# Stick-breaking attention on halves of the TensorE array, with a cap on VectorE for the longest key block

## The reference

```python
z = jnp.einsum('bhqd,bhkd->bhqk', qi, k) * scale
mask = s_idx[None, :] < t_idx[:, None]
log_beta = jax.nn.log_sigmoid(z)
log_one_minus = jnp.where(mask, jax.nn.log_sigmoid(-z), 0.0)
tail = lax.cumsum(log_one_minus, axis=-1, reverse=True) - log_one_minus
a = jnp.where(mask, jnp.exp(log_beta + tail), 0.0)
o = jnp.einsum('bhqk,bhkd->bhqd', a, v)
```

## Time and profile before

| | before |
|---|---|
| median of 3 runs | 1307.05 us (1306.72 to 1307.06) |
| the profiled execution | 1307.16 us, its span 1305.4 us |
| busy in the span: TensorE, VectorE, ScalarE, GpSimd | 98%, 58%, 49%, 26% |
| granted TensorE clock | 0.999 of 2.4 GHz |
| first S to first matmul of `out1` | 501.49 to 626.29 us, 124.80 us |

### The profile page before, as it was taken

One profiled execution on the slowest core, in us unless ns is written; L12 is line 12 of the kernel. 1 busy time (PEld: TensorE's weight loads), 2 busy tenths in 40 slices (PEclk: granted clock), 3 DMA queues, 4 the chain that ended last, 5 costly groups with the idle time before them and its releaser, 6 DMA issues.

```text
span 1305.4 us, 17841 instructions
## 1 busy us (share of the span) xinstructions
PE 1285.4 (98%) x6478; PEld 1072.7 (82%) x6478; DVE 751.5 (58%) x1201; ACT 641.7 (49%) x1164; POOL 344.6 (26%) x393
## 2 busy tenths in 40 slices
PE   7999999999999999999999999999999999999998
PEld 6997778788888888888888888888888888888876
DVE  5656889735652235898454653334475434578843
ACT  5379787724532334998244432513343333357632
POOL 2228877400000007774000000000000000479720
PEclk9999999999999999999999999999999999999999
DMA  5232100122222232001223233332223322321111
GB/s 192 82 113 65 45 19 20 49 97 97 97 97 97 97 97 81 17 0 32 97 97 97 80 98 97 97 97 81 79 87 99 120 97 71 122 78 37 50 65 65
DMA packets 70867, 104.66 MB, mean 80 GB/s; under 512 B 3476, under 2 KB 31368, under 8 KB 70664
## 3 DMA queue, kind: packets, MB, share of 16 engines
q1 hardware_dynamic: 69584, 99.44, 24.2%
q0 software_dynamic: 1088, 4.17, 1.0%
q10 hardware_dynamic: 120, 0.05, 0.0%
HBM read 101.55 MB, written 2.10 MB: 79 GB/s over the span
## 4 chain that ended last, share of the span: by engine, by line
PE 89%; DVE 5%; issue 2%; ACT 2%; DMA 1%; SPq 0%; DVEq 0%; POOL 0%; ACTq 0%; POOLq 0%
PE ps L496 24%; PE ps L498 24%; PE ps L497 24%; PE ps L700 3%; PE ps L858 2%; PE ps L713 1%; PE ps L950 1%; PE ps L679 1%; PE ps L1009 1%; PE ps L848 1%; PE ps L727 1%; PE ps L849 1%; DVE sp L2093 1%; PE ps L728 1%; DMA x_tok<-in_x 1%
## 5 line engine op out<-in xcount | busy, mean ns | idle before, releaser
L1696 DVE TENSOR_TENSOR w_lo<-stage,w_hi 128x1024 fp32r<-128x1024 f32 (+4 forms) x188 | 223.9, 1191 | 416.0 <-ACT w_hi L1115 415.7
L1115 ACT ACTIVATE w_hi<-stage 128x1024 fp32r<-128x1024 f32 (+4 forms) x188 | 191.0, 1016 | 457.8 <-PE ps L498 457.1
L496 PE MATMUL ps<-a0h,w_hi 128*128 128x512 f32 x512 | 203.9, 398 | 1.1 <-DVE q_lo L2280 0.8
L498 PE MATMUL ps<-a0h,w_lo 128*128 128x512 f32 x512 | 199.8, 390 | 0.0
L497 PE MATMUL ps<-a0l,w_hi 128*128 128x512 f32 x512 | 199.5, 390 | 0.0
L2381 POOL TENSOR_TENSOR small<-small 128x16 f32<-128x16 f32 (+2 forms) x14 | 32.3, 2312 | 387.9 <-DVE small L1774 284.4
L496 PE MATMUL ps<-w_hi,a0h 128*128 128x512 f32 (+1 forms) x320 | 121.9, 381 | 0.1
L498 PE MATMUL ps<-w_hi,a0l 128*128 128x512 f32 (+1 forms) x320 | 119.9, 375 | 0.0
L497 PE MATMUL ps<-w_lo,a0h 128*128 128x512 f32 (+1 forms) x320 | 119.8, 374 | 0.0
L496 PEld LDWEIGHTS ps<-a0h,w_hi 128*128 128x128 f32 x512 | 96.2, 188 | 20.8 <-DVE w_lo L1696 1.3
L498 PEld LDWEIGHTS ps<-a0h,w_lo 128*128 128x128 f32 x512 | 96.1, 188 | 20.4
(11 more groups left out here) (331 smaller groups left out, 2807.1 us busy)
## 6 DMA issues: line engine op xcount, KB each, us to landing
stage<-in_a_w_in SPq DMA_DIRECT2D x48, 512.0 KB, 3.7
stage<-in_ple_w_gate SPq DMA_DIRECT2D x16, 512.0 KB, 3.3
stage<-in_w_kv_shared SPq DMA_DIRECT2D x16, 512.0 KB, 3.6
stage<-in_sb_w_in SPq DMA_DIRECT2D x16, 512.0 KB, 3.7
stage<-in_a_w_out SPq DMA_DIRECT2D x16, 512.0 KB, 3.4
stage<-in_b_w_in SPq DMA_DIRECT2D x16, 512.0 KB, 3.7
stage<-in_mla_w_in SPq DMA_DIRECT2D x8, 512.0 KB, 3.8
stage<-in_sb_w_out SPq DMA_DIRECT2D x8, 512.0 KB, 3.3
```

The source lines that it names most:

```text
L496: pe.matmul(bank, wh, mh, start=start and not seeded, stop=False, skip_group_check=seeded)
L498: return pe.matmul(bank, wl, mh, start=False, stop=stop, skip_group_check=seeded)
L1115: act.activation(slab(w_hi[r % 2], L, nk, w), slab(stage[r % 4], L, nk, w), ACT.Copy).then_inc(S("hi_ready"), 1)
L1696: dve.tensor_tensor(slab(w_lo[r % 2], L, nk, w), slab(stage[r % 4], L, nk, w), slab(w_hi[r % 2], L, nk, w), ALU.subtract)\
```

## The change

- **S on row halves.** The split operands go. A block's score is one f32 matmul over 64 rows, and the four blocks of a head alternate between the upper and the lower 64 rows of the array. Two of the four need the head's keys and queries on the other 64 partitions; SyncE copies these by DMA within SBUF (`swap`, four copies of 64x512 a pair). Blocks j=3 and j=2 write the same bank, so j=2 waits for j=3 (`row_done`). The masking matmuls come after all four blocks, two of them merged into one, and each block waits by itself for the W that frees its bank (`a_done` now counts three per head).
- **V on column halves.** Both heads of a pair go into one bank by f32 matmuls with 64 columns of `v_sh` each, the two heads in turn, block by block. V runs once a pair; TensorE's order is T(2i), V(i-1), S(2i+2), T(2i+1), S(2i+3).
- **The cap.** For the longest block ScalarE's abs goes. VectorE writes min(z, 40) (`soft_cap`), ScalarE takes exp(+x) and ln(1+x), and VectorE forms max(min(that, 20), z).
- **Around it.** W waits bank by bank; one gate a pair; the split of its result moves to GpSimd (`sb_parts`), which also issues the loads of `p_tok` and `ws_tok` later; `sp_h` and `sp_l` have two buffers; the loops are written out.

```diff
+EXP_MOST, LOG_MOST = 40.0, 20.0
...
+        def swap(pair):
+
+            if pair < 4:
+                sp_.wait_ge(S("sb_q_read"), pair + 1)
+            if pair > 2:
+                sp_.wait_ge(S("sb_q2_read"), 4)
+            if pair > 1:
+                sp_.wait_ge(S("z_done"), 4 * (pair - 1))
+            for t, to in zip((kT_sh, qT_sb), swapped(pair)):
+                for s in range(2):
+                    sp_.dma_start(to[head_rows(s), :], t[head_rows(s, True), pair, :]).then_inc(S(f"swapped{pair % 2}"), 16)
...
+                    if r == end_load("sb_q2") - 1:
+                        swap(0)
+                        swap(1)
+                    if r == lin["out1"].load0 + 3:
+                        swap(2)
+                    if r == lin["out1"].load0 + 4:
+                        for pair in range(3, PAIRS):
+                            swap(pair)
...
+        def sb_scores(h):
+
+            pair, s = h // 2, h % 2
+            k_other, q_other = swapped(pair)
+            pe.wait_ge(S("sb_q_read"), min(pair + 1, 4))
+            if pair > 3:
+                pe.wait_ge(S("sb_q2_read"), pair - 3)
+            pe.wait_ge(S(f"swapped{pair % 2}"), 64 * (pair // 2 + 1))
+            for n, (j, half) in enumerate(((3, 0), (1, 1), (0, 0), (2, 1))):
                 b, c = KEY_BANK[j]
-                n = T - j * P
-                bank = ps[3 * s + b]
-                kk, qq = slice(j * P, (j + 1) * P), slice(j * P, T)
-                pe.matmul(bank[:, c:c + n], kb[:, kk], qb[:, qq], start=j != 2, stop=False, skip_group_check=True)
-                pe.matmul(bank[:, c:c + n], kb[:, kk], ql[:, qq], start=False, stop=False, skip_group_check=True)
-                t = pe.matmul(bank[:, c:c + P], ident_r[:, :], strict_r[:, :], start=False, stop=False, skip_group_check=True)
-                if j < 2:
-                    t.then_inc(S("z_done"), 1)
-
-        def sb_tails(h, s, first=False):
-
+                rows = head_rows(half)
+                k = kT_sh[rows, pair, j * P:(j + 1) * P] if half == s else k_other[rows, j * P:(j + 1) * P]
+                q = qT_sb[rows, pair, j * P:T] if half == s else q_other[rows, j * P:T]
+                if h > 1 and n < 3:
+                    pe.wait_ge(S("a_done"), 3 * (h - 2) + (n + 1))
+                if j == 2:
+                    pe.wait_ge(S("row_done"), h + 1)
+                t = pe.matmul(ps[3 * s + b][:, c:c + T - j * P], k, q, start=j != 2, stop=False, skip_group_check=True)
+                if j == 3:
+                    t.then_inc(S("row_done"), 1)
+            pe.matmul(two_blocks(ps[3 * s + 2]), ident_r[:, :], twice(strict_r), start=False, stop=False, skip_group_check=True)
+            for b in (1, 0):
+                pe.matmul(ps[3 * s + b][:, 0:P], ident_r[:, :], strict_r[:, :], start=False, stop=False, skip_group_check=True)\
+                    .then_inc(S("z_done"), 1)
+
+        def sb_tails(h, first=False):
+
+            s = h % 2
...
+                if j < MB - 1:
+                    t.then_inc(S("tail_done"), 1)
...
-                t = pe.matmul(ps[6 + s][:, j * P:T], v_pair2[:, j, :], a_T[s][:, KEY_COL[j]:KEY_COL[j] + T - j * P],
-                              start=j == 0, stop=j == MB - 1, skip_group_check=True)
+                for s in range(2):
+                    c = i * P + s * HD
+                    t = pe.matmul(ps[6 + i % 2][head_rows(s), j * P:T], v_sh[:, j, c:c + HD], attend(i, s, KEY_COL[j], T - j * P),
+                                  start=j == 0, stop=j == MB - 1, skip_group_check=True)
             t.then_inc(S("o2_done"), 1)
...
+        for i in range(1, PAIRS):
+            sb_tails(2 * i)
+            sb_values(i - 1)
+            if i < PAIRS - 1:
+                sb_scores(2 * i + 2)
+            sb_tails(2 * i + 1)
+            if i < PAIRS - 1:
+                sb_scores(2 * i + 3)
+        sb_values(PAIRS - 1)
...
+                if p:
+                    break
...
+            done.append(None)
             for p, (_, a, b) in enumerate(PIECES):
-                link.wait(done[p])
-                done[p] = link.mark(act.activation(z[:, a:b], z[:, a:b], ACT.Exp, scale=-1.0))
+                if p:
+                    act.wait_ge(S("capped"), h + 1)
+                else:
+                    link.wait(done[p])
+                done[p] = link.mark(act.activation(z[:, a:b], z[:, a:b], ACT.Exp, scale=1.0 if p else -1.0))
...
+        def weights(h):
+
+            i, s = h // 2, h % 2
+            if i > 1 - s:
+                act.wait_ge(S("o2_done"), i - 1 + s)
+            for n, (b, c, w) in enumerate(((2, 896, 384), (1, T, 384), (0, 0, T))):
+                act.wait_ge(S("tail_done"), 3 * h + n + 1)
+                act.activation(attend(i, s, c, w), ps[3 * s + b][:, 0:w], ACT.Exp).then_inc(S("a_done"), 1)
...
+        for i in range(PAIRS):
+            weights(2 * i)
+            if i == 0:
+                act.wait_ge(S("ring_used"), end_load("sb_q2"))
+                split_to(lin["out1"].load0)
+            if i < PAIRS - 1:
+                soft(2 * i + 2, 0)
+            weights(2 * i + 1)
+            if i < PAIRS - 1:
+                soft(2 * i + 3, 1)
...
+        def soft_cap(h, first=False):
+
+            (bank, c, n), = PIECES[1][0]
+            dve.wait_ge(S("z_done"), 2 * h + 2)
+            at = ps[3 * (h % 2) + bank][:, 0:n]
+            dve.tensor_scalar(soft_parts(h % 2, first)[0][:, c:c + n], at, EXP_MOST, None, ALU.min).then_inc(S("capped"), 1)
+
+        def soft(h, p, first=False):
+
+            s = h % 2
             z, sp_h, sp_l = soft_parts(s, first)
-            for p, (parts_, a, b) in enumerate(PIECES):
-                dve.wait_ge(S("soft_done"), 2 * h + (p + 1))
-                for bank, c, n in parts_:
-                    t = dve.scalar_tensor_tensor(z[:, c:c + n], ps[3 * s + bank][:, 0:n], 0.0, z[:, c:c + n], ALU.max, ALU.add)
-                link(t)
-                if not first and p == 0:
-                    dve.wait_ge(S("tail_done"), h)
-                link(dve.tensor_copy(sp_h[:, a:b], z[:, a:b]))
-                dve.tensor_tensor(sp_l[:, a:b], z[:, a:b], sp_h[:, a:b], ALU.subtract).then_inc(S("sp_done"), 1)
-
-        def sb_pair(i, second=False):
-            a, b = 2 * i, 2 * i + 1
-            soft(a, 0)
-            if not second:
-                o_lo(i - 2, a0h, a0l, "o_sb")
-            o_gate(a - 2, 0, i - 1, ps[6], "o2_done", "o2_read", "o_sb")
-            soft(b, 1)
-            o_gate(a - 1, 1, i - 1, ps[7], "o2_done", "o2_read", "o_sb")
+            parts_, a, b = PIECES[p]
+            dve.wait_ge(S("soft_done"), 2 * h + (p + 1))
+            for bank, c, n in parts_:
+                at = ps[3 * s + bank][:, 0:n]
+                if p:
+                    t = dve.scalar_tensor_tensor(z[:, c:c + n], z[:, c:c + n], LOG_MOST, at, ALU.min, ALU.max)
+                else:
+                    t = dve.scalar_tensor_tensor(z[:, c:c + n], at, 0.0, z[:, c:c + n], ALU.max, ALU.add)
+            link(t)
+            if not first and p == 0:
+                dve.wait_ge(S("tail_done"), 3 * (h - 1))
+            link(dve.tensor_copy(sp_h[:, a:b], z[:, a:b]))
+            dve.tensor_tensor(sp_l[:, a:b], z[:, a:b], sp_h[:, a:b], ALU.subtract).then_inc(S("sp_done"), 1)
+
+        def sb_gated(i):
+
+            dve.wait_ge(S("o2_done"), i + 1)
+            dve.wait_ge(S("act_lo"), i + first_item["o_sb"])
+            dve.tensor_tensor(tmp[0][:, :], ps[6 + i % 2][:, :], sg[:, i, :], ALU.mult).then_inc(S("o2_read"), 1)
...
+        for i in range(1, PAIRS):
+            soft_cap(2 * i)
+            soft(2 * i, 0)
+            soft_cap(2 * i + 1)
+            soft(2 * i, 1)
+            for p in range(2):
+                soft(2 * i + 1, p)
+            sb_gated(i - 1)
+        sb_gated(PAIRS - 1)
 
...
+        def sb_parts(i):
+
+            pool.wait_ge(S("o2_read"), i + 1)
+            pool.tensor_copy(a0h[:, i, :], tmp[0][:, :]).then_inc(S("act_hi"), 1)
+            pool.wait_ge(S("act_hi"), i + (first_item["o_sb"] + 1))
+            pool.tensor_tensor(a0l[:, i, :], tmp[0][:, :], a0h[:, i, :], ALU.subtract).then_inc(S("act_lo"), 1)
+
+        for i in range(PAIRS - 2):
+            sb_parts(i)
```

More of the change, by code:

```diff
@@ L510, in group @@
             if G == lin["out1"].group0 + 1:
[L511 removed]
+                pe.wait_ge(S("o2_read"), PAIRS)
                 pe.wait_ge(S("src_ready"), source(first_item["p1"] + 1))
@@ L1482, in q_twice @@
-        def q_twice(pair, s, kq):
-            q = qT_sb[head_rows(s), pair, :] if isinstance(pair, int) else qT_sb[head_rows(s), bass.ds(pair, 1), :]
-            act.activation(kq[1][s][head_rows(s, True), :], q, ACT.Copy).then_inc(S("q_twice"), 1)
-        def sb_pair(i, first=False, second_last=False, last=False):
-            a, b = 2 * i, 2 * i + 1
-            weights(a, 0, first)
-            if first:
-                act.wait_ge(S("ring_used"), end_load("sb_q2"))
-            sb_values(i, first)
```

(64 more changed lines are left out.)

136 lines of the change are left out of this document (32 added, 104 removed).

## The result

The changed kernel takes 1310.47 us (median of 9 runs, 1309.97 to 1314.14) against 1307.05: a ratio of 1.0032, 95% interval 1.0022 to 1.0042, slower by 3.4 us. The forecast was 1309.4. The runs of before lie within 0.5 us, these within 4.2, and the profiled execution is the longest of them: 1314.14, span 1312.3.

A forecast was written before the change was run, and what follows sets the result against it. The prediction took a loop of one pair through the engines as the bound, 14.31 us against 13.75. Six pairs +3.4, the end -0.7 and the start -0.4 gave +2.3, so 1309.4 us, range 1304 to 1316.

The forecast's parts named there:

- The loop: Dependency round of one pair of heads through TensorE, ScalarE and VectorE, put at 14.31 us against 13.75 before.
- the eight steps: W, one score block, masks, VectorE, block j=0 of T, V, S, ScalarE: together 14.31 us a pair.
- step 7: On TensorE, S of the even head up to its first `z_done`: 1.74 us.
- The end: From T of head 14 to `out1`: 12.35 us where 13.06 pass before, -0.7.
- the start: The stretch ahead of T of head 2, 29.20 us before the change: -0.4.
- Zero-cost items: Work moved or added on ScalarE, GpSimd and the swaps, claimed to cost nothing because waits or spare time cover it.
- step 4: On VectorE, hand-off, the cap, then 0.68, 0.43 and 0.69 with two gaps: 2.51 us.
- A: Rival: mode changes and hand-offs on the loop hide better than drawn; 1303 to 1308 us, chance 0.27.
- B: Rival: TensorE stays the bound, 2.2 us a pair saved over eight pairs; 1289.5 us, chance 0.07.
- the 2.8 of waiting: TensorE's waits per pair, before S of odd heads and before block j=0 of even heads' T: about 2.8 us.
- C: Rival: passes keep program order across halves, S of an even head 0.21 longer; 1311.5 us, chance 0.12.
- D: Rival: row halves run in turn, S of an even head 1.07 longer; 1321.5 us, chance 0.12.

The follow-up runs named there:

- e1: Changed kernel with VectorE's cap of the odd head moved behind the even head's second piece: 1309.43 us.
- e3: Changed kernel with ScalarE's W of the odd head moved between the two logs of the next even head: 1306.72 us.
- e4: Changed kernel with the cap behind the second piece, the first piece's log ahead of the exp awaiting the cap, and W between the two: 1297.10 us.
- e7: Changed kernel with all four score blocks of a head on one row half, so no two run together: 1331.52 us.
- e9: Changed kernel with spare matmuls, whose results nobody reads, filling TensorE's two waits of a pair, the last odd head's included: 1310.44 us.
- e2: Changed kernel with the cap undone, ScalarE taking the longest block's absolute value again, and the halves kept: 1319.85 us.
- e10: e2 with five spare matmuls in TensorE's wait before S of odd heads, the last such wait included: 1304.33 us.
- e8: Changed kernel with the two heads' values issued one head after the other instead of alternating: 1324.83 us.

## Why the prediction was right, and where it was off

**The loop.** From the rows above, one round against the eight steps: W 1.34 (1.37); block and masks, 543.72 to 545.38, 1.66 (1.60); VectorE to 547.89, 2.51 (2.51); block j=0 to V, 1.48 (1.38); V 2.30 (2.28); S to the first `z_done`, 1.72 (1.74); ScalarE 3.47 (3.43). Together 14.48 against 14.31. The moves of e1, e3 and e4 brought the pair to 13.46, 13.96 and 12.59, where the loop said 13.6, 13.95 and 12.7 or under, so its path is shown and not only its length.

**What was mis-sized.** The mask of two blocks, priced at 0.12, takes 0.22 (552.95 to 553.17, and the same for odd heads). And the way into V was counted once, inside V's 2.28; it shows between T and V (0.21 for the usual 0.11), while V's 2.30 holds the way on to S. In step 7 the longer mask is offset, which is luck: what stands ahead of it there took 1.28 (551.67 to 552.95) for 0.14 + 1.07 + 0.05 + 0.14 = 1.40. Over six pairs the 0.165 is 1.0 us. The end, 621.29 to 633.72, took 12.43 for 12.35; the start, 501.64 to 530.74, 29.10 for 28.8. Together that is 1.4 us, somewhat more than the 1.1 by which the median was missed.

**Zero-cost items and rivals.** None of the covered items shows a wait, and VectorE's subtraction takes the 0.69 that step 4 put in. A falls by the 14.48 and the 0.21 before V. B falls by the waits: TensorE is busy 12.23 in a pair of 14.48, and some 0.55 of that lies in the odd head's S, which takes 2.22 instead of 1.67 because its blocks wait one by one for W. With the two waits, 1.2 and 1.1, this comes to about the 2.8 of waiting that the forecast had. The Trainium skill's page TensorEngine Tiling (Array Packing), Overview, promises up to twice the speed; V got 4.26 to 2.30, and the kernel none of it. C falls. In S of head 6, from 552.2 to 552.4:

```profile
551.99 0.59 PE L872 MATMUL ps<-qT_sb,kT_sh 64*128 64x512 f32 x1
552.10 0.48 PE L872 MATMUL ps<-q_swap,k_swap 64*128 64x384 f32 x1
```

The first pass of 512 columns begins at 551.99; the second pass of the 384-column block, earlier in the program, begins at 552.10. S takes 1.67. The Trainium skill's TensorE: Matmul & The Clock Gate, Part 3, has matmuls start strictly in program order; for passes on different halves the rows show otherwise. D falls by e7.

**What the prediction did not see.** Its 2.8 us of waiting a pair were priced at their length alone. In the changed kernel the granted clock falls behind such waits in some runs, for up to 3.7 us in the profiled one. e9 shows that the median owes nothing to it (1310.44 against 1310.47), only the spread. What length of wait is enough isn't settled by these runs, and that it is each wait by itself isn't either: in e3 the waits of 1.1 before j=0 did no harm beside those of 0.7.

## What to carry to other kernels

Where an engine is busy 98% and two others stand close behind, take the round of one period through all engines and add it up, before counting the bound engine's savings: this change took 2 us a pair off V (4.26 to 2.30) and made the pair 0.7 longer, and three moves in the order of ScalarE and VectorE (e4) turned it into a gain of 0.8% over the kernel before. An instruction that waits for the next item must not stand ahead of the current item's last step on an in-order engine. Shortening the work between two waits of TensorE lengthens the waits, and these can cost the clock as well.

## What the runs showed of the hardware

The granted clock of the runs, beside the longest wait before the odd heads' scores in the profiled one: 0.3 and 0.7 us (e4, e3): 0.999 to 1.000; 1.2 (the changed kernel): 0.994 to 0.999; 1.5 (e1): 0.988 to 0.997; 1.6 (e2): 0.983 to 0.992; the same kernel filled to 0.4 (e10): 0.998 to 0.999. The length of this wait isn't all, though: e8 and e7 have the 1.2 of the changed kernel too, and clocks of 0.995 to 0.997 and 0.988 to 0.992. A fall shows as a stretch at 1.2 GHz (some 6.8 us in the changed kernel) that begins up to 2.5 us behind the wait's end (1.9 in the changed kernel), in the middle of work, and costs 1.85 there. The Trainium skill's TensorE: Matmul & The Clock Gate, Part 1 (HAM oscillation), describes such falls where TensorE stands idle for transfers; the two levels agree, and the waits here are for ScalarE and 1.2 to 1.6 us long.
